# A fused two-block transformer kernel: the first unit of keys computed from x before its norm

## What is computed

```python
def rmsnorm(x, g):
    xf = x.astype(jnp.float32)
    ms = jnp.mean(xf * xf, axis=-1, keepdims=True)
    return (xf * lax.rsqrt(ms + EPS) * g.astype(jnp.float32)).astype(x.dtype)

        xn = rmsnorm(h, g_mix_pre[l])
        proj = xn @ w_in[l]
        q = proj[..., :Q_END]
        k = proj[..., Q_END:K_END]
        v = proj[..., K_END:V_END]
        r = proj[..., V_END:R_END]
        a_low = proj[..., R_END:A_END]
```

## Time and profile before

| | us |
|---|---|
| runs of the kernel (3): median, lowest, highest | 1656.02, 1650.72, 1656.76 |
| the profiled execution, its own time | 1655.57 |
| its span | 1653.8 |
| PE (matmul) busy | 1611.8 (97%) |
| DVE busy | 1179.9 (71%) |
| ACT busy | 719.1 (43%) |
| POOL busy | 305.6 (18%) |
| PE's share of the chain that ended last | 76% |

### The profile page before, as it was taken

How to read it: one execution, slowest core, us unless ns; L and a number is a source line. 1 busy time by engine, 2 the same in 40 slices (tenths; PEclk the granted TensorE clock), 3 DMA queues, 4 the chain that set the end, 5 groups by cost and what they waited for, 6 DMA issues and landing times.

```text
span 1653.8 us, 21048 instructions
## 1 busy us (share of the span) xinstructions
PE 1611.8 (97%) x8722; PEld 1316.7 (80%) x8722; DVE 1179.9 (71%) x1636; ACT 719.1 (43%) x931; POOL 305.6 (18%) x211
## 2 busy tenths in 40 slices
PE   7999998999999999999999999999999998999997
PEld 7778787987788898888888899878756877787875
DVE  6998788856443378733565467969567747999998
ACT  5234532347222343212223144443575336777774
POOL 2012000015000010050000001343101005465541
PEclk9999999999999999999999999999999999999999
DMA  7444217852322334453425432223200107999994
GB/s 293 154 159 166 81 54 204 233 173 77 110 94 102 140 115 160 148 192 144 172 90 216 178 109 77 77 77 102 102 26 9 69 8 315 394 397 386 384 381 185
DMA packets 70543, 270.77 MB, mean 164 GB/s; under 512 B 23968, under 2 KB 32800, under 8 KB 43952
## 3 DMA queue, kind: packets, MB, share of 16 engines
q1 hardware_dynamic: 45280, 163.31, 27.9%
q0 software_dynamic: 15696, 101.87, 15.5%
q10 hardware_dynamic: 9472, 4.26, 1.0%
HBM read 244.00 MB, written 25.41 MB: 163 GB/s over the span
## 4 chain that ended last, share of the span: by engine, by line
PE 76%; DVE 15%; ACT 4%; DMA 3%; POOL 1%; issue 1%; SPq 1%; DVEq 0%; ACTq 0%; POOLq 0%
PE bank L394 75%; DVE wsplit L2879 4%; DVE parts L2879 4%; DMA ring<-in_wmoe,indices 1%; ACT wsplit L1158 1%; DVE wsplit L1881 1%; DMA block<-xslot 1%; ACT g_high L1423 1%; DVE hidden L2903 0%; POOL r_row L2991 0%; DMA cst<-in_cst 0%; DVE block_out L2921 0%; PE bank L933 0%; PE bank L607 0%; SPq L3192 0%
## 5 line engine op out<-in xcount | busy, mean ns | idle before, releaser
L1881 DVE TENSOR_TENSOR wsplit<-ring,wsplit 128x2048 fp32r<-128x2048 f32 x82 | 189.9, 2316 | 154.1 <-ACT wsplit L1158 153.9
L394 PE MATMUL bank<-h_high,wsplit 128*128 128x512 f32 (+1 forms) x992 | 290.6, 376 | 0.4 <-DVE h_low L2543 0.3
L1158 ACT ACTIVATE wsplit<-ring 128x2048 fp32r<-128x2048 f32 x93 | 177.6, 1912 | 175.7 <-PE bank L394 168.4
L394 PE MATMUL bank<-xn_high,wsplit 128*128 128x512 f32 (+1 forms) x832 | 216.0, 346 | 0.2 <-DVE gla_state L2219 0.2
L394 PEld LDWEIGHTS bank<-h_high,wsplit 128*128 128x128 f32 x992 | 180.8, 188 | 36.6 <-DVE h_low L2543 0.5
L394 PE MATMUL bank<-h_low,wsplit 128*128 128x512 f32 (+1 forms) x496 | 184.9, 373 | 0.0
L394 PE MATMUL bank<-f_high,wsplit 128*128 128x512 f32 (+1 forms) x576 | 173.2, 380 | 0.2 <-DVE wsplit L1881 0.2
L394 PEld LDWEIGHTS bank<-xn_high,wsplit 128*128 128x128 f32 x832 | 144.7, 189 | 20.6 <-issue 1.3
L394 PE MATMUL bank<-xn_low,wsplit 128*128 128x512 f32 (+1 forms) x416 | 137.4, 344 | 0.0
L394 PEld LDWEIGHTS bank<-f_high,wsplit 128*128 128x128 f32 x576 | 107.4, 192 | 20.3 <-DVE wsplit L1881 0.4
L394 PEld LDWEIGHTS bank<-h_low,wsplit 128*128 128x128 f32 x496 | 93.3, 188 | 17.4 <-issue 0.2
(11 more groups left out here) (540 smaller groups left out, 3328.0 us busy)
## 6 DMA issues: line engine op xcount, KB each, us to landing
ring<-in_W SPq DMA_DIRECT2D x122, 1024.0 KB, 4.9
weights_out<-prep SPq DMA_DIRECT2D x8, 864.0 KB, 7.8
prep<-weights_out_early POOLq DMA_DIRECT2D x8, 576.0 KB, 3.1
toeplitz<-kpad SPq DMA_DIRECT2D x128, 32.0 KB, 3.2
xslot<-zeros SPq DMA_DIRECT2D x7, 516.0 KB, 5.0
block<-xslot SPq DMA_DIRECT2D x6, 516.0 KB, 11.9
yslot<-block_out SPq DMA_DIRECT2D x6, 512.0 KB, 8.8
prep<-turns_early POOLq DMA_DIRECT2D x8, 288.0 KB, 2.5
```

Source lines behind the costliest of these rows:

```text
L394: return g.matmul(o, l, r, start=first, stop=last_, skip_group_check=True)
L1158: g.activation(split_in(n, 0), ringt[:, n % RING, :], ACT.Copy).then_inc(*a.sig(("high", n)))
L1881: g.tensor_tensor(split_in(n, 1), ringt[:, n % RING, :], hi, SUB).then_inc(*t.sig(("low", n), ("released", n)))
```

## The change

1. SyncE's first loads are reordered: the gain of the norm (8 columns of `vecs`) alone first, then x part pairs 0 and 1, k0's weights in two halves between them (one behind x's first pair, one behind its third), then x's last pair, the constants, k1's weights, the rest of `vecs`.
2. Unit k0 is multiplied with x * gain, without the token's scale. Its high part is made by ScalarE (`x_gain_high`), its low part by VectorE (`x_gain_low`), all 8 parts on VectorE. k0's results are copied to `KR` (`k_raw`), and VectorE multiplies them with the scale (`rstd`), two TENSOR_TENSOR of 128 x 528.
3. The sum over partitions for the norm stands in TensorE's order between parts 6 and 7 of k0, the spreading of the scale behind k0. `keep_busy` is gone.
4. ScalarE copies the scale from PSUM to SBUF (`rst`), and VectorE forms the normed x with one SCALAR_TENSOR_TENSOR to each part, from SBUF.
5. k1 is done part by part of the normed x, as k0 was. k1's weights are split before the normed x, not behind it, and ScalarE's four copies of k0's results stand before the normed x instead of among the SSM's sines.

```diff
@@ linear @@
-                if each and i == 0:
+                if each and (i == 0 or name == "k"):
                     p.wait_ge(*at("low_part", 0) if n == 0 else at("low", n))
...
             halves = [(n, xnh[:, :, lo:hi], xnl[:, :, lo:hi]) for n, (lo, hi) in enumerate(HALVES)]
...
-            p.wait_ge(cst_landed, 16)
-            keep_busy(4)
-            b = fresh("ms")
-            p.wait_ge(*at("ms", "square"))
-            for m, lo in enumerate((0, 128, 256, 384, 400)):
-                t = mm(b[:, m:m + 1], sq[:, 0, lo:lo + 128], ones[:, 0:1], m == 0, m == 4)
-            t.then_inc(*p.sig(("ms",)))
-            banks.close("ms")
-            keep_busy(2)
+            raw = [(n, xuh[:, :, lo:hi], xul[:, :, lo:hi]) for n, (lo, hi) in enumerate(HALVES)]
+            def norm_rows(k):
+                if k == 5:
+                    b = fresh("ms")
+                    p.wait_ge(cst_landed, 16)
+                    p.wait_ge(*at("ms", "square"))
+                    for m, lo in enumerate((0, 128, 256, 384, 400)):
+                        t = mm(b[:, m:m + 1], sq[:, 0, lo:lo + 128], ones[:, 0:1], m == 0, m == 4)
+                    t.then_inc(*p.sig(("ms",)))
+                    banks.close("ms")
+            linear("k", 0, raw, each="xu", beside=norm_rows)
             b, b2 = fresh("ms", "scale"), fresh("ms", "tail")
...
-            keep_busy(8)
-            for i in range(2):
-                linear("k", i, halves, each="xn")
+            linear("k", 1, halves, each="xn")
@@ scalar @@
             for k in range(8):
                 a.wait_ge(x_landed[k // 2], 16)
+                g.activation(xuh[:, k, :], HT0[:, k, :], ACT.Copy, scale=vec("g_mix_pre")[:, k:k + 1]).then_inc(*a.sig(("xu_high", k)))
+                if k == 0:
+                    high_part(0, 0)
+                if k == 4:
+                    high_part(0, 1)
                 if k > 3:
                     a.wait_ge(*at("sq_added", k - 3))
...
+            high_part(1, 0)
+            high_part(1, 1)
             a.wait_ge(cst_landed, 16)
...
-            high_part(0, 0)
-            high_part(0, 1)
+            copies("k", 0, 2, 2, lambda j, c: KR[:, j, slice(*HALVES[c])])
+            a.wait_ge(*at("ms", "scale"))
+            g.activation(rst[:, 0:512], banks.at("ms", "scale"), ACT.Copy).then_inc(*a.sig(("free", "ms", "scale")))
+            g.activation(rst[:, 512:NT], banks.at("ms", "tail")[:, 0:NT - 512], ACT.Copy).then_inc(*a.sig(("free", "ms", "tail"), ("token_scale",)))
             for k in range(8):
                 a.wait_ge(*at("xn_value", k))
                 g.activation(xnh[:, k, :], HT0[:, k, :], ACT.Copy).then_inc(*a.sig(("xn_high", k)))
-                if k in (3, 5):
-                    high_part(1, k // 4)
...
-            copies("k", 0, 2, 2, lambda j, c: K[:, j, slice(*HALVES[c])])
@@ vector @@
-            for k in range(1, 8):
-                v.wait_ge(*at("sq", k))
-                v.wait_ge(*v.own())
-                g.tensor_tensor(sq[:, 0, :], sq[:, 0, :], sq[:, 1 + (k - 1) % 3, :], ADD).then_inc(*v.sig(("sq_added", k), ("ms", "square")))
+            for k in range(8):
+                v.wait_ge(*at("xu_high", k))
+                g.scalar_tensor_tensor(out=xul[:, k, :], in0=HT0[:, k, :], scalar=vec("g_mix_pre")[:, k:k + 1], in1=xuh[:, k, :].bitcast(F32),
+                                       op0=MUL, op1=SUB).then_inc(*v.sig(("xu", k)))
+                if k == 0:
+                    low_part(v, g, 0, 0)
+                else:
+                    v.wait_ge(*at("sq", k))
+                    v.wait_ge(*v.own())
+                    g.tensor_tensor(sq[:, 0, :], sq[:, 0, :], sq[:, 1 + (k - 1) % 3, :], ADD).then_inc(*v.sig(("sq_added", k), ("ms", "square")))
             v.wait_ge(*at("root", "ms"))
             g.reciprocal(rt5, rt5).then_inc(*v.sig(("inverse", "ms")))
-            low_part(v, g, 0, 0)
-            v.wait_ge(*at("ms", "scale"))
+            next_low("k", 0)
+            v.wait_ge(*at("token_scale"))
             for k in range(9):
                 if k < 8:
-                    for w, c in (("scale", slice(0, 512)), ("tail", slice(512, NT))):
-                        g.scalar_tensor_tensor(out=HT0[:, k, c], in0=HT0[:, k, c], scalar=vec("g_mix_pre")[:, k:k + 1],
-                                               in1=banks.at("ms", w)[:, 0:c.stop - c.start], op0=MUL, op1=MUL).then_inc(
-                            *v.sig(("xn_value", k), ("free", "ms", w)))
+                    g.scalar_tensor_tensor(out=HT0[:, k, :], in0=HT0[:, k, :], scalar=vec("g_mix_pre")[:, k:k + 1],
+                                           in1=rst, op0=MUL, op1=MUL).then_inc(*v.sig(("xn_value", k)))
                 if k % 2:
...
-            next_low("k", 0)
+            v.wait_ge(*at("k_out", 1, 1))
+            v.wait_ge(*at("xn", 1))
+            v.wait_ge(*v.own())
+            for j in range(2):
+                g.tensor_tensor(K[:, j, :], KR[:, j, :], rst, MUL).then_inc(*v.sig())
```

More of the change, by code:

```diff
@@ L179, in program @@
         iota_landed = semaphore("iota_landed")
+        first_landed, gain_landed = semaphore("first_landed"), semaphore("gain_landed")
         (vecs_landed, cst_landed, wal_landed, wgu_landed, bc_landed, pos_landed, route_landed, slots_cleared,
@@ L234, in program @@
         zt = tile("zeros", 36376, ROW)
+        xuh, xul = tile("x_gain_high", 16208, 8, NT, dt=F32R), tile("x_gain_low", 20432, 8, NT, dt=F32R)
+        KR = tile("k_raw", 25488, 2, NT)
         K, LA = tile("k", 0, 4, NT), tile("log_a", 2112, 4, NT)
@@ L423, in linear @@
                 per = size // nk // 128
-                if each and i == 0:
+                if each and (i == 0 or name == "k"):
                     p.wait_ge(*at("low_part", 0) if n == 0 else at("low", n))
-                    grown = [(j, tag, xh, xl, fresh(name, j, tag)[:, 0:xh.shape[2]]) for j in range(per) for tag, xh, xl in cuts]
+                    grown = [(per * i + j, m, tag, xh, xl, fresh(name, per * i + j, tag)[:, 0:xh.shape[2]]) for j in range(per) for m in (slice(128 * j, 128 * j + 128),) for tag, xh, xl in cuts]
                     for k in range(nk):
@@ L430, in linear @@
                             p.wait_ge(*at("low_part", 1))
-                        for j, tag, xh, xl, b in grown:
-                            m = slice(128 * j, 128 * j + 128)
+                        for j, m, tag, xh, xl, b in grown:
                             t = three(b, wh[:, k, m], wl[:, k, m], xh[:, k, :], xl[:, k, :], k == 0, k == nk - 1)
@@ L437, in linear @@
                             beside(k - 1)
-                    for j, tag, *_ in grown:
+                    for j, _, tag, *_ in grown:
                         banks.close(name, j, tag)
@@ L452, in tensor @@
             xr = [(0, xnh[:, :, 16:NT], xnl[:, :, 16:NT])]
-            idle = fresh("idle")
-            def keep_busy(n):
-                for _ in range(n):
-                    t = mm(idle[:, 0:128], ones, ident, True, True)
-                t.then_inc(*p.sig(("free", "idle")))
-            p.wait_ge(cst_landed, 16)
-            keep_busy(4)
-            b = fresh("ms")
-            p.wait_ge(*at("ms", "square"))
-            for m, lo in enumerate((0, 128, 256, 384, 400)):
-                t = mm(b[:, m:m + 1], sq[:, 0, lo:lo + 128], ones[:, 0:1], m == 0, m == 4)
-            t.then_inc(*p.sig(("ms",)))
-            banks.close("ms")
-            keep_busy(2)
+            raw = [(n, xuh[:, :, lo:hi], xul[:, :, lo:hi]) for n, (lo, hi) in enumerate(HALVES)]
[9 more added lines that the diff above has]
+            linear("k", 0, raw, each="xu", beside=norm_rows)
             b, b2 = fresh("ms", "scale"), fresh("ms", "tail")
@@ L477, in tensor @@
             banks.close("ms", "tail")
-            keep_busy(8)
-            banks.close("idle")
-            for i in range(2):
-                linear("k", i, halves, each="xn")
+            linear("k", 1, halves, each="xn")
             for h, (lo, hi) in enumerate(HALVES):
@@ L1188, in high_part @@
                 w = slice(1024 * z, 1024 * z + 1024)
-                a.wait_ge(*landed(n))
+                if (n, z) == (0, 0):
+                    a.wait_ge(first_landed, 16)
+                else:
+                    a.wait_ge(*landed(n))
                 g.activation(wst[:, side(n), 0, w], ringt[:, n % RING, w], ACT.Copy).then_inc(*a.sig(("high_part", n, z), ("high", n)))
@@ L3136, in loads, with load_x @@
                     load(n)
-            for i in range(4):
+            def load_x(i):
                 g.dma_start(HT0[:, 2 * i:2 * i + 2, :], xT[:, 2 * i:2 * i + 2, :]).then_inc(x_landed[i], 16)
+            g.dma_start(vt[:, 0:8], vecs[:, 0:8]).then_inc(gain_landed, 16)
+            load_x(0)
+            g.dma_start(ringt[:, 0, 0:1024], W[0][:, 0:1024]).then_inc(first_landed, 16)
+            load_x(1)
+            load_x(2)
+            g.dma_start(ringt[:, 0, 1024:2048], W[0][:, 1024:2048]).then_inc(ring_landed[0], 16)
+            load_x(3)
```

(3 more changed lines are left out.)

6 lines of the change are left out of this document (3 added, 3 removed).

## The result

The changed kernel takes 1660.89 us (median of 8 runs, 1659.65 to 1664.81) beside 1655.21 for the kernel before (8 runs, 1650.72 to 1656.76): ratio 1.0045, 95% interval 1.0034 to 1.0056, slower by 0.45%. The forecast was 1666.0 in 1657.0 to 1669.5. The range holds the time; the half per cent that I gave 0.60 was just missed, and the time lies in "within", to which I gave 0.38. The same kernel measured once more (e8) gave 1.0061, 1.0048 to 1.0075. The two intervals overlap from 1.0048 to 1.0056, on the very bound. The profiled execution took 1664.81, against a sum of 1666.0 that was made for one such execution; among the first eight it is the slowest, among the five of e8 the profiled one (1665.95) is the second slowest.

What follows compares the result with a forecast made beforehand. TensorE, busy 97%, was taken as the bound, with VectorE feeding v0 at 2.88 us margin. v0's delay of 7.8 plus half clock 2.6 made +10.4 on 1655.57: 1666.0 us, range 1657.0 to 1669.5.

Steps and rivals of the forecast that it cites:

- the half per cent: Whole kernel: slower by over 0.5%, above 1664.3 us, chance 0.60.
- within: Whole kernel: time within 0.5% (8.3 us) of the kernel before, chance 0.38.
- the first rival: Normed products on VectorE aren't held by GpSimd; only one of four collisions is paid: +6.4, 1662.0 us, chance 0.16.
- TensorE's start and the scale: Kernel start: k0 begins at 8.9, slow at first; squares summed at 21.5; normed x begins at 26.7.
- The collisions: Normed x to `wal_low`: GpSimd holds four VectorE instructions with SBUF operands, 1.34 each, 5.4 us in all.
- The rest of the stage: Normed x to `wal_low` without collisions: products, differences, first wait, `wal_low` and k_raw times scale, 9.25 us.
- The parameters: `wal_low` to v0's split on VectorE: unchanged except -0.7 for ScalarE's copies moved from before the last sine; split ends 57.0.
- The half clock: At v0: after standing still for 9.2 us, TensorE comes back at half clock, +2.6 us.
- the two terms: v0 waits for its weights until 57.0, +7.8 us; TensorE's half clock after that wait, +2.6 us.
- which changes nothing at this size: Whole kernel: the profiled execution lies 0.45 us below the median 1656.02, taken as not mattering to the sum.
- TensorE's path decides: At v0: if its weights are split when a_low ends, the early k0 counts: 1652.5 us, chance 0.04.
- The delay is lost again: Behind 150 us: stages where other engines end the chain absorb the delay: 1655.6 us, chance 0.06.

Runs made afterwards that it cites:

- e8: Changed kernel measured again with nothing edited, with a second profile: 1663.05 us, ratio 1.0061.
- e1: Changed kernel with the normed products taking the token's scale from PSUM again, 512 and 16 tokens separately: 1660.76 us, ratio 1.0039.
- e5: Changed kernel with the low parts of all eight normed parts on VectorE, none on GpSimd: 1659.28 us, ratio 1.0043.
- e2: Changed kernel with 60 unread matmuls between a_low and TensorE's wait for v0's weights: 1661.5 us, ratio 1.0048.
- e3: Changed kernel with v0's weights split ahead of the SSM's parameters on ScalarE and VectorE: 1662.66 us, ratio 1.0056.
- e7: Kernel before with only the change's order of loads; norm, products and keys as before: 1658.27 us, ratio 1.003.
- e6: Changed kernel, scale from PSUM, all low parts on VectorE, v0's, v1's and v2's splits and a_low's copy moved earlier: 1661.24 us, ratio 1.0054.

## Why the prediction came out as it did

The range held, and the mechanism with it: VectorE is late, v0 waits for it, the clock falls. The size is another matter. The forecast was +10.4; the medians of the first series lie 5.7 apart (plain means 7.3), those of e8's batch 9.8 (10.5), all runs with a recorded clock 9.0 in the mean. The prediction calls its lower end, 1657, "just below the first rival", but that rival stands at 1662.0; the measured 1660.89 lies in these 5 us, which no term of the prediction fills. That this series fell so low is in part luck: its runs of the kernel before have their median at 1655.21, those of the four other batches at 1653.0 to 1654.4.

**TensorE's start and the scale: right.** k0 at 9.34 (8.9 expected), slow at first for some 4.6 us (5.3), squares summed at 21.96 (21.5), sum by TensorE 22.10 (22.0), normed x at 26.67 (26.7).

**The collisions: right in kind, too large.** Four instructions were held, but three of them products and one the scaling of the keys, by 1.83 - 0.76 = 1.07 and 1.83 - 0.70 = 1.13 each, not by 1.34: 4.3 instead of 5.4. The number of four was right; what was mis-sized is the price of one. GpSimd lost 0.4 to 0.5 as well. The rest of the stage took 9.8 instead of 9.25. `wal_low` ended at 40.76 (41.4 expected). The Trainium skill, "SBUF — State Buffer", Who interferes with whom, has the whole instruction excluded. The trace agrees (the product held at 28.77 ends 0.56 after GpSimd's difference), and e1 (PSUM operand, 0.74) and e5 (no partner, 0.76) agree that it needs both sides. I had left the first rival (products not held) 0.16; the earlier trace rows should have brought it lower.

**The parameters.** From the end of `wal_low` to v0's split it is 12.73 us (before 13.95): -1.2, where I took -0.7 for the copies of the keys; the rest is a TENSOR_SCALAR of 128 x 32 on `ssm_small` that took 0.67 before, with GpSimd's MEMSET of `zeros` beside it, and takes 0.18 now. So v0 began at 55.83, not 57.0, and the delay was 6.7 instead of 7.8.

**The half clock: right in kind, its worth in the runs smaller.** v0 to the gates lost 2.8 in the profiled execution (2.6 expected), and e2 shows that the idle time is the cause. Two things the forecast didn't have: the slow stretch behind the gates grew as well (gates to kernels(0) 21.03 instead of 19.41, of which the gates 1.1 and v2 0.5; it is 19.54 in e2 and, at a granted clock of 1.00 from 80 to 100, 17.84 in e5), and 1.9 came back between there and the end (the granted clock is 0.68 in 975 to 985 and 0.83 in 1380 to 1390 before; in the changed kernel it is 0.83 at its lowest near 990, and 1.00 from 1380 to 1410). Over all runs, the mean clock is 0.0029 lower than before, worth 1.9 us at 0.65 for each 0.001; the remaining 7.0 are near the lateness of v0 (6.7). So the two terms, 7.8 + 2.6 in the sum, came out at about 7 + 2. The first was mis-sized by the price of a held product (-1.1, of which the rest of the stage took back 0.5) and by the parameters (-0.5). The second is an estimate from the fit, good to some 0.8 us. The sentence that failed is "which changes nothing at this size", on the profiled execution's place among the runs: the changed kernel's two profiled executions lie 2.3 and 1.5 us above the fitted line (residuals 1.0 rms), so the sum, made for a profiled execution, came close to these two (1664.81, 1665.95) and not to the median.

**The rivals.** "TensorE's path decides" needed v0's split to end by 46.0. e3 brought that about (43.23), and it did not help: v1's weights, the gates' copies and the SSM's parameters were late in their turn. Had the rival's condition been met in the change, its 1652.5 would still have been wrong. "The delay is lost again" did not happen: e7's shift of 4 us comes out at the end, and 9.2 of the changed kernel's 11.1.

**Where the norm's 9.2 us come from.** Before, VectorE had the squares summed at 8.49 + 3.15 = 11.64:

```profile
8.49 3.15 DVE L1911 TENSOR_TENSOR squares<-squares 128x528 f32<-128x528 f32 x4 [0.34 <-ACT squares L1198]
```

With the new loads alone it is 15.42 (e7), with the whole change 21.96. So the loads account for 3.8, what VectorE does between the sums for the other 6.5 (eight products for `x_gain_low` and half a weight split, one of the eight held for 2.96 instead of 0.76 beside GpSimd's half split), and 1.1 comes back between the sum and the normed x. This is read from three traces; neither part was taken out of the changed kernel by itself.

**In one line:** 12 us of k0 were taken off TensorE's order, but the norm starts 9.2 us later, mostly because the gained x costs VectorE eight products more; VectorE has next to no slack before kernels(0), so what counts is its delay.

**Open:** whether the profiled executions of the changed kernel really pay more for the clock than the others (two of 13 runs), which no run could show, since only profiled ones show where the clock was low; and why the same idle time before k1 was followed by half clock in one of its two traces and not in the other.

## What to carry to other kernels

Before work is started earlier on the busiest engine, follow the engine that feeds it through the whole stretch: if that has no idle time either, its added instructions decide, and a cure at the first wait moves the wait to the next unit. An operand moved from PSUM to SBUF can cost more than the instruction that it saves, where GpSimd reads SBUF beside it. Under 1% compare the mean granted clock of the runs with their times before a mechanism of a few microseconds is read out of a median; but where the change itself moves the clock, a comparison at equal clock hides what it did. And two cures that each gain alone can undo each other: measure them together against each of them.

## What was not expected of the hardware

- GpSimd's subtractions in VectorE's stretch (1.34 alone) made VectorE slower than doing all eight itself, where its products had both operands in SBUF: 3.05 us a pair of parts with them, 2.60 without. With one operand in PSUM it was the other way round: 2.22 with them (e1), 2.84 without (e6).
- The kernel's time follows its mean granted clock, 0.65 us for each 0.001, and that clock ranged from 0.986 to 0.992 over the 13 runs of the changed kernel.
